# Heads of an attention turned between its steps, and the decay's root and scans moved

## What is computed

```
q = (rms_norm(c_q) @ w_uq) ; kv = (rms_norm(c_kv) @ w_ukv)     # per head
q, k = rms_norm per head, rope on the last 64 dimensions
s = q k^T * 192**-0.5, causal ; p = softmax(s) ; o = p v       # in 2 blocks of 128 queries

r, i = sigmoid(xc @ w_rg + b), sigmoid(xc @ w_ig + b)
log_a = -8 * r * softplus(-lam) ; a = exp(log_a)
mult  = sqrt(-expm1(2 * log_a)) ; b = mult * i * xc
h_t = a_t * h_(t-1) + b_t                                      # scan over the 256 tokens
rec = gelu(y_gate) * h
x = x + concat(rms_norm(o), rms_norm(rec)) @ w_out
x = x + peer_ffn(rms_norm(x))                                  # gathers rows of two tables
```

## Time and profile before

| | |
|---|---|
| median of 3 runs | 2747.48 us (2737.89 to 2752.47) |
| the profiled execution | 2738.01 us |
| its span, first to last instruction | 2736.2 us |
| mean granted clock of TensorE | 0.886 of full |
| busy: TensorE, VectorE, ScalarE, POOL | 71%, 73%, 21%, 38% |
| DMA over the span | 324 GB/s |

### The profile page before, as it was taken

One profiled execution on the slowest core, in us unless ns is written; L12 is line 12 of the kernel. 1 busy time (PEld: TensorE's weight loads), 2 busy tenths in 40 slices (PEclk: granted clock), 3 DMA queues, 4 the chain that ended last, 5 costly groups with the idle time before them and its releaser, 6 DMA issues.

```text
span 2736.2 us, 20692 instructions
## 1 busy us (share of the span) xinstructions
PE 1948.3 (71%) x7632; PEld 1337.3 (49%) x7632; DVE 1984.6 (73%) x2497; ACT 569.0 (21%) x830; POOL 1051.8 (38%) x648
## 2 busy tenths in 40 slices
PE   8998999459204777777775000049899889899997
PEld 5776458455101223222222000049788778688885
DVE  6887886988896765444445999989664759777666
ACT  3044100010000000100001000023434343545343
POOL 0011003455486555544545888820065550000000
PEclk9999999779657999999999555569999999999998
DMA  9672978989999999999999999977743439777552
GB/s 377 233 283 77 356 283 345 393 330 421 422 422 422 421 421 422 422 421 422 422 421 421 422 422 422 422 277 289 279 154 123 152 141 350 280 292 284 202 202 104
DMA packets 123508, 887.60 MB, mean 324 GB/s; under 512 B 13840, under 2 KB 14352, under 8 KB 16528
## 3 DMA queue, kind: packets, MB, share of 16 engines
q0 software_dynamic: 80640, 587.24, 52.0%
q1 hardware_dynamic: 39024, 276.58, 27.2%
q10 hardware_dynamic: 3744, 22.47, 2.1%
HBM read 884.13 MB, written 2.10 MB: 324 GB/s over the span
## 4 chain that ended last, share of the span: by engine, by line
PE 38%; DMA 23%; POOL 16%; DVE 16%; issue 4%; ACT 2%; ACTq 0%; DVEq 0%; SPq 0%
PE psum L776 21%; DMA W<-in_peer_v,W 17%; POOL W L644 10%; POOL early_rows L644 7%; PE psum L708 6%; PE psum L732 4%; PE psum L970 3%; DMA W<-in_peer_u,W 3%; DVE split L1751 1%; DMA early_rows<-in_peer_u,W 1%; DVE early_rows L2073 1%; PE psum L921 1%; PE psum L1021 1%; DMA ring<-in_w_even 1%; DMA XN<-in_ada 1%
## 5 line engine op out<-in xcount | busy, mean ns | idle before, releaser
L776 PE MATMUL psum<-split,hi 128*128 128x512 f32 x1664 | 519.7, 394 | 18.0 <-DVE split L1751 8.6
L2073 DVE CUSTOM_DVE_ANT_0 W<-W,XN 128x2048 f32<-128x2048 f32 x147 | 333.9, 2291 | 214.5 <-DMA W<-in_peer_u,W 213.7
L1202 ACT ACTIVATE split<-ring 128x1024 fp32r<-128x1024 f32 x272 | 283.4, 1057 | 427.4 <-PE psum L776 312.0
L1751 DVE TENSOR_TENSOR split<-ring,split 128x1024 fp32r<-128x1024 f32 x208 | 251.7, 1232 | 146.3 <-ACT split L1202 145.3
L776 PEld LDWEIGHTS psum<-split,hi 128*128 128x128 f32 x1664 | 314.6, 190 | 86.0 <-issue 14.9
L970 PE MATMUL psum<-W,HT 128*128 128x512 f32 x616 | 282.3, 601 | 96.5 <-DMA W<-in_peer_v,W 96.5
L970 PE MATMUL psum<-early_rows,HT 128*128 128x512 f32 x408 | 193.2, 618 | 214.8 <-ACT HT L1411 149.3
L2073 DVE CUSTOM_DVE_ANT_0 early_rows<-early_rows,XN 128x2048 f32<-128x2048 f32 x109 | 247.3, 2291 | 136.1 <-DMA early_rows<-in_peer_u,W 134.6
L644 POOL DMA_INDIRECT W<-in_peer_v,W x153 | 280.3, 1832 | 159.9 <-PE psum L970 127.8
L644 POOL DMA_INDIRECT W<-in_peer_u,W x147 | 205.3, 1396 | 142.4 <-DVE W L2073 56.7
L670 POOL TENSOR_TENSOR split<-ring,split 128x1024 fp32r<-128x1024 f32 x64 | 158.2, 2492 | 244.0 <-ACT split L1202 244.0
(11 more groups left out here) (366 smaller groups left out, 3121.5 us busy)
## 6 DMA issues: line engine op xcount, KB each, us to landing
ring<-in_ada SPq DMA_DIRECT2D x48, 1024.0 KB
ring<-in_odd SPq DMA_DIRECT2D x48, 1024.0 KB
XN<-in_ada POOLq DMA_DIRECT2D x21, 1024.0 KB, 9.6
early_rows<-in_ada POOLq DMA_DIRECT2D x16, 1024.0 KB, 7.8
ring<-in_w_out SPq DMA_DIRECT2D x16, 1024.0 KB
ring<-in_pq SPq DMA_DIRECT2D x16, 1024.0 KB
ring<-in_c_k SPq DMA_DIRECT2D x16, 1024.0 KB
ring<-in_c_v SPq DMA_DIRECT2D x16, 1024.0 KB
```

The source lines that it names most:

```text
L776: m = nc.tensor.matmul(dst, lhs, rhs, start=(k == 0 and b == 0 and not (features and i % 2)), stop=(k == KD - 1 and b == 2 and not (featur ...
L1202: A(split[:, 2048 * (n % PIECES):2048 * (n % PIECES) + 1024], ring[:, at:at + 1024], ACT.Copy)\
L1751: TT_(split[:, to + 1024:to + 2048], ring[:, at:at + 1024], split[:, to:to + 1024], ALU.subtract)\
L2073: V.tensor_tensor_reduce(out=row, in0=row, in1=xn3[:, tt, :], scale=1.0, scalar=0.0, op0=ALU.mult, op1=ALU.add, accum_out=PACT[:, c:c + 1])\
```

## The change

Four edits. (1) The two decay passes on VectorE go from behind the second token half of the norms into it, right after its rstd; ScalarE takes the root ahead of the first two Gelus. (2) Six scans run ahead of the first heads' copies, one in step 0 and one in step 1. (3) TensorE turns three heads (QK_TURNED), and starts the steps; in the even steps 0 to 8, after the score, it turns one more head each. ScalarE and VectorE copy two heads (QK_COPIED) ahead of the steps and one in each even step 0 to 10: ScalarE after the exponential, VectorE after the maximum. The scores wait for the heads one by one. The plan numbers the units in the new order. (4) VectorE copies a head's rotated q and k with one instruction instead of two, into another layout of XN (`qk_rope`; its name QRT and KRT stay for the scores, as slices of the same memory).

```diff
--- before.py
+++ after.py
@@ -51,6 +51,8 @@
 ROWS = 10
 REC_STEP = 11
 
+QK_TURNED, QK_COPIED = 3, 2
+
 
 
 
@@ -229,11 +231,15 @@
     p.gemm("ukv", 4, 1, 2, 1024)
     p.units("gates", 8)
     p.gemm("in_y", 2, 4, 2, 2048)
-    p.units("qkT", 16)
+    p.units("qkT", 2 * QK_TURNED)
     for step in range(2 * NH + 2):
         for name, lag in (("score", 0), ("probT", 1), ("pv", 2)):
             if 0 <= step - lag < 2 * NH:
                 p.unit[name, step - lag] = len(p.unit)
+            h = step // 2 + QK_TURNED
+            if name == "score" and step % 2 == 0 and h < NH:
+                for i in (2 * h, 2 * h + 1):
+                    p.unit["qkT", i] = len(p.unit)
         if step == REC_STEP:
             p.units("rec_ss", 1)
     for c in range(4):
@@ -849,7 +855,8 @@
             feature_gemm("in_y", 2, ht)
 
             pe.wait_ge(sem("qk_ready"), TT)
-            for h in range(NH):
+
+            def qk_turn(h):
                 for i, (n, qs, ks) in enumerate(((DN, lambda tt: qr4[:, tt, h, 0:DN], lambda tt: kv4[:, tt, h, 0:DN]),
                                                  (DR, lambda tt: qr4[:, tt, h, DN:DQ], lambda tt: kr4[:, tt, h, :]))):
                     o = open_unit(("qkT", 2 * h + i))
@@ -857,18 +864,23 @@
                         for tt in range(TT):
                             m = nc.tensor.transpose(o[0:n, a * S + tt * P:a * S + (tt + 1) * P], src(tt), IDENT)
                     close(m, ("qkT", 2 * h + i))
-            pe.wait_ge(sem("qkT_act"), NH)
-            pe.wait_ge(sem("qkT_dve"), NH)
+
+            for h in range(QK_TURNED):
+                qk_turn(h)
             for step in range(2 * NH + 2):
                 i = step
                 if i < 2 * NH:
                     h, tt = i // 2, i % 2
                     nk = P * (tt + 1)
+                    pe.wait_ge(sem("qkT_act"), h + 1)
+                    pe.wait_ge(sem("qkT_dve"), h + 1)
                     o = open_unit(("score", i))
                     nc.tensor.matmul(o[:, 0:nk], QT[:, h, tt * P:(tt + 1) * P], KT[:, h, 0:nk], start=True, stop=False)
                     m = nc.tensor.matmul(o[:, 0:nk], QRT[:, h, tt * P:(tt + 1) * P], KRT[:, h, 0:nk],
                                          start=False, stop=True)
                     close(m, ("score", i))
+                    if tt == 0 and h + QK_TURNED < NH:
+                        qk_turn(h + QK_TURNED)
                 i = step - 1
                 if 0 <= i < 2 * NH:
                     pe.wait_ge(sem("prob_ready"), i + 1)
@@ -1265,15 +1277,15 @@
                     m = A(YG[:, 2 * S * i:2 * S * i + 2 * S], bank(("in_y", i)), ACT.Gelu)
                     give(m, ("in_y", i))
 
-            gelus(0)
             act.wait_ge(sem("mult_sq"), 1)
             A(TMP, TMP, ACT.Sqrt).then_inc(sem("mult_ready"), 1)
+            gelus(0)
             gelus(1)
             for i in (2, 3):
                 gave(act, ("in_y", i))
             act.sem_inc(sem("yg_ready"), 1)
 
-            for h in range(NH):
+            def qk_copy(h):
                 wait_unit(act, ("qkT", 2 * h))
                 src = bank(("qkT", 2 * h))
                 seq(A(QT[:, h, :], src[:, 0:S], ACT.Copy, scale=column("hq")))
@@ -1304,10 +1316,14 @@
                 m = A(AO[:, i % 2, (i // 2) * P:(i // 2 + 1) * P], bank(("pv", i))[:, 0:P], ACT.Copy, scale=st(80 + i))
                 give(m, ("pv", i))
 
+            for h in range(QK_COPIED):
+                qk_copy(h)
             for step in range(2 * NH + 2):
                 for fn, lag in ((exps, 0), (prob_T, 1), (att_out, 2)):
                     if 0 <= step - lag < 2 * NH:
                         fn(step - lag)
+                    if fn is exps and step % 2 == 0 and step // 2 + QK_COPIED < NH:
+                        qk_copy(step // 2 + QK_COPIED)
                 if step == REC_STEP + 1:
                     act.wait_ge(sem("rec_ms"), 1)
                     A(TMP[:, 0:S], TMP[:, 0:S], ACT.Sqrt).then_inc(sem("rec_rms"), 1)
@@ -1876,6 +1892,11 @@
                 seq(V.tensor_reduce(st(60), SQ[:, 1024:1088], AX.X, ALU.add))
                 seq(TS(st(52, 8), st(52, 8), st(60), None, ALU.add))
                 rstd(st(44, 16), st(44, 16), DQ, EPS, 168)
+                if tt == 1:
+                    dve.wait_ge(sem("tanh_ready"), 8)
+                    dve.wait_ge(sem("decay_sq"), 1)
+                    seq(STT(TMP, TMP, 1.0, RR, ALU.add, ALU.mult))
+                    TS(TMP, TMP, 1.0e-30, None, ALU.max).then_inc(sem("mult_sq"), 1)
                 seq(TS(st(104 + 8 * tt, 8), st(44, 8), DQ ** -0.5, None, ALU.mult))
                 z = q[:, :, DN:DQ]
                 seq(TT_(z, z, over_heads(heads_g[:, DN:DQ], DR), ALU.mult))
@@ -1886,25 +1907,29 @@
                 seq(TT_(kr, over_heads(raw, DR), wide(st(52, 8), DR), ALU.mult))
                 dve.sem_inc(sem("qk_ready"), 1)
 
-            dve.wait_ge(sem("tanh_ready"), 8)
-            dve.wait_ge(sem("decay_sq"), 1)
-            seq(STT(TMP, TMP, 1.0, RR, ALU.add, ALU.mult))
-            TS(TMP, TMP, 1.0e-30, None, ALU.max).then_inc(sem("mult_sq"), 1)
+            def scans(first, last):
+                for j in range(first, last):
+                    a = slice(S * j, S * j + S)
+                    seq(V.tensor_tensor_scan(XC[:, a], GA[:, a], TMP[:, a], 0.0, ALU.mult, ALU.add))
+                if last == 8:
+                    dve.sem_inc(sem("scan_done"), 1)
+
             dve.wait_ge(sem("mult_ready"), 1)
             dve.wait_ge(sem("ix_ready"), 1)
             seq(TT_(TMP, TMP, II, ALU.mult))
-            for j in range(8):
-                a = slice(S * j, S * j + S)
-                seq(V.tensor_tensor_scan(XC[:, a], GA[:, a], TMP[:, a], 0.0, ALU.mult, ALU.add))
-            dve.sem_inc(sem("scan_done"), 1)
-            for h in range(NH):
+            scans(0, 6)
+            qk_rope = XN[0:DR, :].rearrange("p (a h s) -> p a h s", a=2, h=NH)
+
+            def qk_copy(h):
                 wait_unit(dve, ("qkT", 2 * h + 1))
                 src = bank(("qkT", 2 * h + 1))
-                seq(V.tensor_copy(QRT[:, h, :], src[0:DR, 0:S]))
-                m = V.tensor_copy(KRT[:, h, :], src[0:DR, S:2 * S])
+                m = V.tensor_copy(qk_rope[:, :, h, :], src[0:DR, :].rearrange("p (a s) -> p a s", a=2))
                 give(m, ("qkT", 2 * h + 1))
                 gave(dve, ("qkT", 2 * h + 1))
                 dve.sem_inc(sem("qkT_dve"), 1)
+
+            for h in range(QK_COPIED):
+                qk_copy(h)
 
             def ao_squares(i):
 
@@ -1927,6 +1952,10 @@
                     gave(dve, ("score", i))
                     V.tensor_reduce(st(64 + i), SC[:, i % 2, 0:nk], AX.X, ALU.max, negate=True)\
                         .then_inc(sem("score_ready"), 1)
+                    if i % 2 == 0 and i // 2 + QK_COPIED < NH:
+                        qk_copy(i // 2 + QK_COPIED)
+                    if i < 2:
+                        scans(6 + i, 7 + i)
                 i = step - 1
                 if 0 <= i < 2 * NH:
                     dve.wait_ge(sem("prob_ready"), i + 1)
```

## The result

The changed kernel takes 2750.06 us (median of 20 runs, 2744.45 to 2758.42). The kernel before, run beside it 20 times, takes 2744.05 us (2737.89 to 2752.47). The ratio is 1.0019, with a 95% interval of 1.0010 to 1.0028: about 5 us slower, within what was called no change (0.5%). The forecast was 2.8 us slower. The profiled execution of the changed kernel took 2747.19 us (span 2745.4, mean granted clock 0.882); that of the kernel before took 2738.01 (2736.2, 0.886). So the profiles differ by 9.2 us and the medians by 6.0, and part of the difference between the profiles is of the executions that happened to be profiled.

A forecast was written before the change was run, and what follows sets the result against it. The prediction took a chain of waits along VectorE, the attention steps and TensorE as the bound. Step 0 10.75 us sooner against 13.56 us more in the steps gave 2.8 us later: 2747.5 + 2.8 = 2750.3 us, range 2738 to 2762.

The forecast's parts named there:

- Ahead of the steps: Edits to root, scans and copies before the attention steps: step 0 at 229.35 instead of 240.10, 10.75 us sooner.
- the forecast for step 0: First attention step on TensorE: start at 229.35 us, after head 0's copy at 229.2 and 0.15 us handover.
- The second half: Second token half on VectorE: ends some 3.6 us later, hidden because the heads' transposes wait for the gate product; 0 cost.
- The moved table load: ScalarE: one table load goes, a 1.28 us row under the gate product; taken as 0, at most 0.2 us gained.
- Banks: Attention steps: late emptying of reused banks stops TensorE; steps take 31.56 us instead of 18.00, 13.56 more.
- The pair at full clock: Two attention steps, even score to even score: 6.27 us instead of 3.42.
- The rival of the free banks: Attention steps: banks do not stop TensorE; 7.7 us gained, 2739.8 us; chance 0.15.
- its price per pair: Free-banks rival, attention steps: a turned head costs 0.55 us in each of four even steps.
- The clock: Rival: TensorE's clock falls to 1.2 GHz during the steps; 16 us more for five pairs, 2766 us; chance 0.12.
- the forecast of the output product: Output product after the steps: start near 281.7 us, the 2.8 us delay at step 11 carried on.
- The full price of a pair: Clock rival, attention steps: some 3.2 us more for a pair at 1.2 GHz.
- The base: Whole kernel before the change: 2747.5 us, median of three runs, to which 2.8 us was added.

The follow-up runs named there:

- the second look: Kernel before and changed kernel, each unchanged and profiled once more; these executions took 2744.32 us (before) and 2747.18 us (changed).
- the doubled copy: Changed kernel with the first of ScalarE's two copies of heads 3 to 7 made twice; 2756.59 us, ratio to before 1.0034.
- edit 1 undone: Changed kernel with the decay passes and the order of root and Gelus as before; 2753.54 us, ratio to before 1.0030.
- the spread scans: Version with both engines copying each head in its turning step, but three scans ahead and one in each of steps 0 to 4; 2738.99 us, ratio to before 0.9977.
- the one with edit 1 alone: Kernel before with only the decay passes moved into the second token half and the root ahead of the first Gelus; 2745.12 us, ratio 0.9997.
- The version with all copies earlier: Changed kernel with ScalarE and VectorE both copying later heads at the end of the even step that turned them; 2731.72 us, ratio to before 0.9947.
- The version with all copies earlier and edit 1 undone: Both engines copying each head in its turning step, decay passes and root order as before; 2735.98 us, ratio to before 0.9964.
- the version with earlier copies: Changed kernel with both ScalarE and VectorE copying each later head in the step that turned it; 2731.72 us, ratio to before 0.9947.

## Why the prediction was right, and where it was not

**Ahead of the steps: right.** The transposes began at 224.07, 0.97 us sooner than at 225.04, since the gate product ended sooner in this execution; VectorE, on which step 0 waits, was ahead by as much (the norms ended at 220.65, forecast 221.6). Shifted by 0.97, the forecast for step 0 is 228.38, and it started at 228.38. The multiply came at 220.87 (shifted forecast 220.8), the copy of 64 x 512 took 0.67 (row in step 0, forecast 0.69). The second half was covered: nothing in front of the transposes. The moved table load showed no gain: the last Gelus now wait 4.84 us for the gate product, and step 0 waits for VectorE.

**Banks: right, in place and size.** The count named the standstill in step 2 at the value product, in steps 4, 6 and 8 at the transposes, and in step 10 at the turned probabilities. There they are: 1.94, 2.28, 2.16, 2.27 and 2.37 us. The pair at full clock took 6.21 us (forecast 6.27), score 4 came at 237.53 (shifted forecast 237.50). Copies in the step in which the head was turned took the standstills away, and a longer copy lengthened them. The rival of the free banks is so refuted for this kernel, and its price per pair was right for the kernel in which the banks are free.

**The clock: the failed step.** It was a rival at 0.12, priced as all or nothing: 3.2 us in each of five pairs. The rows read against it (1.00 after the standstill in 238 to 240 us) were one execution's; in the second look at the same kernel the clock fell to 0.52 after the same standstill. It came in part: two of the pairs took 1.7 us more than forecast each and the way to score 11 0.4 more, 3.84 us in all from score 4 to score 11 (26.28 instead of 22.44). After score 11 the clock was at 0.52 in 262 to 266, and the sum of squares took 4.56 us where it took 3.62 in before; the stretch to score 12 cost 2.43 us that the forecast had taken as unchanged. 3.84 and 2.43, less the 0.97 by which this execution was ahead at step 0, are 5.30 of the 5.34 us between the forecast of the output product (279.13 + 2.8 = 281.93) and 287.27. The text put the product near 281.7, which was 0.2 too low by its own sum. In the second look the same two terms were 7.02 us (29.46 from score 4 to score 11) and 2.63. The full price of a pair was right: 3.2 us, the 3.7 of the doubled copy less the copy's 0.50. What was wrong is that the forecast itself held none of it. The Trainium skill, "TensorE: Matmul & The Clock Gate", section "A second HAM failure mode: psum-queue depth-cycling", tells of such a swing between the two levels in another kernel that cycles through the banks; the rows here agree, and the two looks at the changed kernel show it in stretches of different length.

**The base: wrong by 3.4 us the other way.** The median of three runs, 2747.48, stood for the kernel before; 20 runs give 2744.05. The change was forecast 3.2 us too small (2.8 against 6.0 by the medians, 5.2 by the ratio). The two errors cancel, so that 2750.3 against 2750.06 says more of luck than of the sum. The mechanism and the sign are what was right.

**What stays open.** Which execution loses its clock, and where, I can't say from rows: in the kernel before it happened within the steps in one of two looks. The kernels with five standstills of 1.93 to 2.75 us in the steps lost it there in every look (the changed one twice, edit 1 undone, the doubled copy), and the spread scans lost it after their 3.06 us; the others kept it from 242 to 254 us, all but the kernel before and the one with edit 1 alone, which stand still ahead of the steps. The version with all copies earlier and edit 1 undone stands still there too (4.37 us) and lost it from 230 to 238 us only. That is an association over thirteen profiled executions, and no run held the clock and varied the standstills. The output product starts 15.25 us later in the changed kernel than in the version with earlier copies: 0.34 of it is there at score 4, 8.64 are the banks at full clock (22.44, as forecast, less the 13.80 measured from score 4 to score 11), 6.27 the clock (3.84 and 2.43). The last term is read from rows, not tried by itself. The medians differ by 3 us more than the product's starts, and that, as the 3 us between executions behind the product's start, is not explained.

## What to carry to other kernels

When results share a fixed rotation of banks, count the units: the instruction that empties a bank must be issued, on its engine, before the work that depends on the unit that takes the bank next. Here the start 11.7 us sooner was lost to five releases issued late and to the slower clock behind them, and issuing them at the end of the step in which the head was turned made some 5 us lost into 13 us won. Price a standstill of TensorE with the slower work behind it as well as with its own length, and take the base of a small change from many runs and two profiles, not from three runs and one.

## What the hardware showed that was not expected

**A VectorE instruction with two inputs in SBUF waited out POOL's product, at up to 17 times its price.** A sum of squares of 128 x 128 takes 0.27 us, and 4.57 us beside POOL's product. It was in the kernel before already, in another stage (VectorE's timeline, then POOL's):

```profile
179.03 2.35 DVE L1737 CUSTOM_DVE_ANT_0 XN<-XN,early_rows,col 128x2048 f32<-128x2048 f32 x1
...
181.31 6.08 DVE L1871 TENSOR_TENSOR W<-W 128x1536 f32<-128x1536 f32 x1
...
201.88 1.76 DVE L1871 TENSOR_TENSOR W<-W 128x1536 f32<-128x1536 f32 x1
```

```profile
179.85 5.91 POOL L617 TENSOR_TENSOR W<-W 128x2048 f32<-128x2048 f32 x1
```

The first of two equal instructions at L1871 began while POOL's ran, until 185.76, and took 4.3 us longer than the second. It goes the other way round too, as far as one row can say: POOL's product began while VectorE's instruction of L1737, which reads two tiles, ran (until 181.38) and took 5.91 us, where its product of the same size in the steps takes 4.52. Moving these was not tried. VectorE's copies out of PSUM stayed at 0.67 us beside POOL.

**One kernel's clock falls in different stretches from one execution to the next.** Two profiled executions of one kernel began the output product 4.4 us (before) and 3.4 us (after) apart, nearly all of it between scores at 1.2 GHz. The kernel before spreads over 14.6 us and the changed one over 14.0 (20 runs each). Three versions without standstills in the steps spread over 2.2, 4.7 and 8.0 us (6 runs each), but the doubled copy, with five standstills, over 7.5 (8 runs). That the spread goes with the standstills is so not shown.
